# Attention blocks transposed three steps behind their scores instead of two, over four score buffers, with the low part of the transposed output subtracted one step later

## What is computed

```
o_i = softmax(scores of pattern i) @ v         for (window, dilation) in ((128,1), (512,4), (2048,16))
o   = sum_i softmax_i(lse_i) * o_i             weights s_i / sum_j s_j, s_i the softmax denominators
mix = concatenate([attn, silu(layernorm(dwconv31(a * sigmoid(g))))])
x   = x + mix @ w_out
```

## Time and profile before

| | |
|---|---|
| median of 3 runs | 2429.41 us |
| the profiled execution's own time | 2427.01 us |
| its span in the trace | 2425.2 us |
| TensorE (PE) busy | 2377.7 us, 98% |
| VectorE (DVE) busy | 1547.7 us, 64% |
| ScalarE (ACT) busy | 790.5 us, 33% |
| attention stage, from the first score to the last read of a transposed output | 251.4 to 395.4 us in the first layer, 1455.8 to about 1599.5 us in the second |

### The profile page before, as it was taken

The page is one execution under the profiler, slowest core; times in us unless marked ns, Lnnn a source line. Parts: engine busy times, 40 slices in busy tenths (PEclk is TensorE's granted clock), DMA queues, the critical chain, the costliest instruction groups (busy, mean ns, idle before and its releaser), DMA issues.

```text
span 2425.2 us, 30715 instructions
## 1 busy us (share of the span) xinstructions
PE 2377.7 (98%) x11672; PEld 1945.6 (80%) x11672; DVE 1547.7 (64%) x1659; ACT 790.5 (33%) x1050; POOL 157.0 (6%) x57
## 2 busy tenths in 40 slices
PE   7999999999999999999999998999999999999999
PEld 6888777888888888888778887778888888888887
DVE  5999774665555555555749997756555555555555
ACT  4322674432222222222332227754322222222221
POOL 0122001100000000000102120011000000000000
PEclk9999999999999999999999999999999999999999
DMA  4323531121111111111112244301211111111111
GB/s 159 88 79 114 144 81 36 44 61 52 35 52 52 52 43 52 43 52 43 43 35 79 79 139 114 79 18 53 61 53 44 48 39 52 52 51 44 46 49 70
DMA packets 46676, 153.44 MB, mean 63 GB/s; under 512 B 7424, under 2 KB 10112, under 8 KB 46592
## 3 DMA queue, kind: packets, MB, share of 16 engines
q1 hardware_dynamic: 45728, 149.93, 21.3%
q10 hardware_dynamic: 864, 2.36, 0.2%
HBM read 131.02 MB, written 21.23 MB: 63 GB/s over the span
## 4 chain that ended last, share of the span: by engine, by line
PE 88%; issue 5%; DVE 3%; ACT 2%; POOLq 0%; DMA 0%; DVEq 0%; POOL 0%; SPq 0%; ACTq 0%
PE mm L484 60%; PE aux L484 20%; PE aux L642 3%; PE aux L623 2%; PE mm L596 2%; PE aux L511 1%; DVE y L1191 1%; ACT sc L926 1%; ACT pT_large L940 0%; PE aux L520 0%; DMA x<-xT 0%; POOLq L1499 0%; DVE x_lo L1117 0%; PE aux L577 0%; DVE w_lo L1105 0%
## 5 line engine op out<-in xcount | busy, mean ns | idle before, releaser
L484 PE MATMUL mm<-x_hi,w_hi 128*128 128x512 f32 x1952 | 609.4, 393 | 17.5 <-DVE x_lo L1117 11.5
L484 PE MATMUL mm<-x_hi,w_lo 128*128 128x512 f32 x1952 | 604.5, 391 | 0.0
L484 PE MATMUL mm<-x_lo,w_hi 128*128 128x512 f32 x1952 | 604.1, 391 | 0.0
L484 PEld LDWEIGHTS mm<-x_hi,w_hi 128*128 128x128 f32 x1952 | 363.9, 188 | 97.0 <-issue 12.4
L484 PEld LDWEIGHTS mm<-x_lo,w_hi 128*128 128x128 f32 x1952 | 366.9, 188 | 79.6
L484 PEld LDWEIGHTS mm<-x_hi,w_lo 128*128 128x128 f32 x1952 | 366.7, 188 | 79.0
L793 ACT ACTIVATE w_hi<-w_raw 128x1024 fp32r<-128x1024 f32 x154 | 161.9, 1058 | 659.1 <-PE mm L484 461.2
L1111 DVE TENSOR_TENSOR x<-x,aux 128x1024 f32<-128x1024 f32 x176 | 214.8, 1221 | 121.2 <-PE aux L484 111.6
L1105 DVE TENSOR_TENSOR w_lo<-w_raw,w_hi 128x1024 fp32r<-128x1024 f32 x154 | 196.6, 1282 | 54.0 <-ACT w_hi L793 50.0
L1123 DVE TENSOR_TENSOR uv<-mm,rinv 128x1024 f32<-128x1024 f32 x44 | 53.9, 1225 | 220.3 <-PE mm L484 220.1
L1191 DVE SCALAR_TENSOR_TENSOR y<-u_all,cpar,y 128x512 f32<-128x512 f32 x248 | 186.6, 765 | 0.1
(11 more groups left out here) (190 smaller groups left out, 2938.9 us busy)
## 6 DMA issues: line engine op xcount, KB each, us to landing
w_raw<-weights SPq DMA_DIRECT2D x188, 512.0 KB, 3.6
qk_scratch<-m SPq DMA_DIRECT2D x64, 128.0 KB, 2.1
qk_scratch<-o SPq DMA_DIRECT2D x64, 128.0 KB, 2.1
x_hi<-qk_scratch SPq DMA_DIRECT2D x32, 256.0 KB, 6.4
q_first<-qk_scratch SPq DMA_DIRECT2D x8, 512.0 KB, 4.6
k_hh_first<-qk_scratch SPq DMA_DIRECT2D x16, 256.0 KB, 6.0
k_ll_first<-qk_scratch SPq DMA_DIRECT2D x16, 256.0 KB, 6.5
x_hi<-qk_scratch SPq DMA_DIRECT2D x8, 512.0 KB, 4.8
```

What stands on the lines that cost most here:

```text
L484: last = pe.matmul(acc[:, cols], a, b[:, cols], start=start and n == 0, stop=stop and n == 2)
```

## The change

Everything that follows the exponential moves one step later against the scores: transposes of step n - 3 run in step n, the attends at r6, r0, r2, r4, the h fill and `read_out` at r7, `move_out` at r4, the o fills at r1 and r3. The stage has 76 steps instead of 75. The order of the fills, and with it the bank of each, stays. `add_mask(n)` writes `sc[n % 4]` and waits for the transposes of step n - 4. The four buffers have the widths of the widest step that uses them (3, 7, 4 and 8 blocks, 22 in all; before, three of 8). On VectorE alone the subtraction into `x_lo` is done one step later still, after the next step's `add_mask` and tap.

```diff
-O_AT = 24
-H_AT = 14
+O_AT = 25
+H_AT = 15
-ATTENDS = ((5, 0, 2), (7, 3, 3), (9, 1, 6), (11, 2, 7))
-LAST_STEP = STEPS + 11
+ATTENDS = ((6, 0, 2), (8, 3, 3), (10, 1, 6), (12, 2, 7))
+LAST_STEP = STEPS + 12
...
-        if 2 <= n < STEPS + 2:
-            qb = BLOCKS[(n - 2) % TB]
+        if 3 <= n < STEPS + 3:
+            qb = BLOCKS[(n - 3) % TB]
             for a in range(0, qb + 1, 4):
-                fills.append((n, "p", n - 2, a, min(a + 4, qb + 1)))
+                fills.append((n, "p", n - 3, a, min(a + 4, qb + 1)))
...
-        sc = [sb(f"sc{i}", [P, SEQ], to=attn) for i in (2, 0, 1)]
+        widest = [(max(BLOCKS[i], BLOCKS[i + 4]) + 1) * P for i in range(4)]
+        sc = [sb(f"sc{i}", [P, widest[i]], to=attn) for i in (3, 0, 1, 2)]
         sc = sc[1:] + sc[:1]
...
-                        blocks = [sc[which % 3][:, kb * P:(kb + 1) * P] for kb in range(a, z)]
+                        blocks = [sc[which % 4][:, kb * P:(kb + 1) * P] for kb in range(a, z)]
...
-                    if n == STEPS + 4:
+                    if n == STEPS + 5:
...
-                    if n == STEPS + 7:
+                    if n == STEPS + 8:
...
-                    if n >= 11 and (n - 11) % TB == 0 and n < STEPS + 11:
-                        move_out((n - 11) // TB)
+                    if n >= 12 and (n - 12) % TB == 0 and n < STEPS + 12:
+                        move_out((n - 12) // TB)
...
-                    if n >= 3:
-
-                        dve.wait_ge(pt_full, at(l, PT, LAST_FILL[n - 3] + 1))
+                    if n >= 4:
+
+                        dve.wait_ge(pt_full, at(l, PT, LAST_FILL[n - 4] + 1))
...
-                for n in range(LAST_STEP):
+                for n in range(LAST_STEP + 1):
...
                     for f in range(PT):
-                        if FILLS[f][0] == n:
+                        if FILLS[f][0] == n - 1:
                             read_turn(f)
```

More of the change, by code:

```diff
@@ L920, in exps @@
                     h, qb = n // TB, BLOCKS[n % TB]
-                    s = sc[n % 3][:, 0:(qb + 1) * P]
+                    s = sc[n % 4][:, 0:(qb + 1) * P]
                     act.wait_ge(mm_read, at(l, MM, M_SCORE + n + 3))
@@ L1313, in add_mask @@
                     dve.wait_ge(mm_full, at(l, MM, M_SCORE + n + 1))
-                    if n == 2:
+                    if n == 3:
                         dve.wait_ge(qk_stored, at(l, QK_STORES, QK_STORES + 16))
-                    if n >= 3:
-                        dve.wait_ge(pt_full, at(l, PT, LAST_FILL[n - 3] + 1))
+                    if n >= 4:
+                        dve.wait_ge(pt_full, at(l, PT, LAST_FILL[n - 4] + 1))
                     plain(dve)
-                    dve.tensor_tensor_reduce(sc[n % 3][:, 0:keys], mm[n % 2][:, 0:keys],
+                    dve.tensor_tensor_reduce(sc[n % 4][:, 0:keys], mm[n % 2][:, 0:keys],
                                              logcount[:, SEQ - keys:SEQ], -SCALE, 3e38, ALU.add, ALU.min,
```

## The result

The changed kernel took 2407.41 us (median of 4 runs, 2406.41 to 2409.03) against 2429.1 for the kernel before: 21.7 us less, ratio 0.9914 (95% interval 0.9902 to 0.9927). Forecast were 2412.3 and a range of 2406 to 2421.5. The executions of the kernel before fall into two groups, 2426.6 to 2427.6 and 2428.5 to 2430.5 us, and three of the four behind 2429.1 are of the upper one, so the 20.2 us between the two profiled executions is the safer figure.

What follows compares the result with a forecast made beforehand. TensorE was taken as the bound (88% of the span), so only its waits could be won: 8.2 us per layer in the stretches, plus 0.75 tail, less 0.4 start, 17.1 in both, giving 2412.3 us, range 2406 to 2421.5.

Steps and rivals of the forecast that it cites:

- The waits for exponentials, 1.06 per head: TensorE's waits of 0.32 and 0.74 us at the transposes in each head vanish; head falls from 15.79 to 14.73.
- The 0.07 at k0: Wait of TensorE at k0 for ScalarE's copy of the r2 transposes, 0.07 us per head, bounds 0 and 0.5.
- both paths: From the last issue of scores at r3 to k0: ScalarE's path 5.46 us, TensorE's own 5.45, called level.
- o heads 15.7: Heads with two o fills take 15.7 us instead of 17.47, bounds 15.6 and 16.6.
- Head 3 17.6 with one transpose waiting 1.9: Subtraction queues behind a tap stretched to 2.75 us, so TensorE waits 1.9; head 3 takes 17.6 instead of 18.72.
- The GpSimd sum in head 1, 0.4 lost: Stretched tap of r6 delays the mask of r7 and read_out: 0.4 us lost once per layer, bounds 0 to 1.0.
- Start, 0.4 lost: k1 of head 0 stands behind the first scores of head 1: 0.4 us lost per layer, bounds 0 to 1.
- Tail, 0.75 gained: The 1.31 us wait for the last exponential goes, transposes queue 0.56 for ScalarE's copies: 0.75 gained, bounds 0 to 1.31.
- The sum: Seven stretches fall from 116.8 to 108.6 us; with tail and start, 8.55 gained per layer, 17.1 in both.
- B: Rival: ScalarE's copy before k0 sets every head, 0.5 us in 16 heads, 8 us less gain, 2420.3; chance 0.17.
- C: Rival: lead does not grow, exponential waits return as waits of scores; 2.8 us gained, 2426.6; chance 0.12.
- D: Rival: turn bank held too long by the late subtraction, TensorE waits at transposes; 23.8 us, 2436.1; chance 0.06.

Runs made afterwards that it cites:

- e7: Changed kernel with one more ScalarE copy of 128x512 per head, just ahead of move_out, into a tile nothing reads: 2411.8 us, ratio 0.9934 to before.
- e4: Changed kernel with the three GpSimd sums all waiting for the last tap of the last tile: 2402.8 us, ratio 0.9898 to before.
- e6: Changed kernel with the subtraction two steps after its o fill instead of one: 2443.6 us, ratio 1.0062 to before.
- e1: Changed kernel with the subtraction back in the step of its o fill, lag of three and four buffers kept: 2412.4 us, ratio 0.9936 to before.
- e2: Kernel before with only the subtraction one step later, lag of two and three buffers kept: 2423.1 us, ratio 0.9981 to before.
- e3: Changed kernel with the three full-width score buffers of before, the mask waiting for transposes of step n - 3: 2422.4 us, ratio 0.9977 to before.

## Why the prediction was right, point by point

- *The waits for exponentials, 1.06 per head.* Right: a plain head was to be 14.73 plus 0.07 and is 14.69 to 14.72. The 0.07 at k0 was not there; e7 shows that there is less than 0.1 to spare. From the last issue of `scores` at r3 (271.74) to k0 (277.04) it is 5.30, where both paths had been summed to 5.45 and 5.46: over-estimated by 0.15, and level as forecast.
- *o heads 15.7.* Measured 15.75 in head 5 of the first layer and 15.99 in the second, against 17.47 before. The 15.51 of head 7 is partly luck of the cut: 0.24 of it is the scores of a next head, which the sum did not take out.
- *Head 3 17.6 with one transpose waiting 1.9.* 17.56, and 1.77 for that transpose, where 1.9 was forecast; e4 shows the stretched tap as the cause.
- *The GpSimd sum in head 1, 0.4 lost.* Mis-sized: 0.10 (14.82 to 14.72 in e4), though the tap was stretched to 2.49.
- *Start, 0.4 lost.* Wrong in sign, and so was the sign to look for, a first k1 some 0.4 later: from the first score to the first k1 it took 13.36 and takes 13.24. The scores ahead of k1 do cost 0.4 (264.43 to 264.84), but the forecast left out that an exponential is waited for here too. TensorE's waits there were 1.37 for a mask and 1.06 for an exponential, and are 1.47, 0.28 and 0.41, all for masks: 0.3 less. The other 0.3 that it takes to come out ahead was not traced.
- *Tail, 0.75 gained.* Mis-sized: from the last k1 to the first matmul after the subtraction 13.83 became 12.67, 1.16 gained. From the start of the last fifteen transposes to the attend behind them it was 3.30 (383.50 to 386.80, with the wait of 1.31) and is 2.15 (374.51 to 376.66), which is the whole of it. Weight loads wait 0.38 for ScalarE's copy there; the forecast had 0.56. What is left of the miss is that a wait shown as 1.31 costs about 1.5 from start to start.
- *The sum.* It was 8.55 per layer and came out at 9.07 for the stretches (116.84 to 107.77), 0.12 at the start and 1.16 in the tail, 10.35; in the second layer 8.84, 0.11 and 1.17, 10.12. That is 20.5 us where 17.1 were forecast. The miss is the last three terms (0.3 + 0.5 + 0.4 per layer) and, in the first layer, 0.35 in the plain heads and 0.14 in the o heads, all to the same side. The median missed by more, 4.9 us: on the scale of the profiled execution it was 3.1 (2409.9 against 2406.8), and the 2.4 added from there to the median was 0.6 this time.
- *Rivals.* B needed 0.5 per head at k0 and found none, but e7 shows how near it was. C is out: scores in plain heads wait for no mask. (Its price had a slip: 7 of 8.55 lost leaves 1.55 per layer, 3.1 us and 2426.3, not 2.8 and 2426.6; no chance hangs on it.) D is out for this change, and e6 shows that it is real one step further: slower than the kernel before.

- *The parts.* I summed lag and postponement as if the one's worth did not hang on the other. For the sum it made no difference, since both were in my list; e1 and e2 show that in the o heads 5 and 7 either alone brings little.

Head 5 of the second layer took 15.99, where the first layer's took 15.75. There the transposes of r2 also waited for the bank: the scores ahead of them start at 1531.09 and the transposes at 1532.12, 1.03 apart, where head 1 has 0.78. The forecast had that bank free 0.1 before it is asked for. The delay comes from further ahead: in the second layer the mask of r3 starts 1.64 after its scores begin (1526.65 to 1528.29) and in the first 1.41 (332.95 to 334.36), and exponential, copy and subtraction behind it are late by as much. VectorE was idle before that mask in both; why it starts later in one layer stays open.

## What to carry to other kernels

When TensorE waits in the middle of a software pipeline, first list what each step holds (score buffer, PSUM bank, a place in an engine's list), since a resource given back later may cost nothing up to a point and then more than its own wait: here the subtraction one step late cost next to nothing except in head 3, two steps late 36 us. A deeper lag may want a further buffer, the more so where something else on the same engine is postponed; here three buffers instead of four cost 4 us alone and 15 with it. And once the slack is used, look again at contention that was covered before: moving three GpSimd sums was worth 2.5 us ahead of the change and 3.8 after it.

## What the hardware showed that was not expected

TensorE's clock fell after some waits of about 2 to 3 us. In head 3 of e6, after 2.91 us of waiting, the granted clock was 0.68 of full speed in the next 1.7 us and 0.54 in the 2.5 behind (near the lower of its levels, 1.2 and 2.4 GHz), and the k3 attend took 1.1 us longer. After 1.77 us in the changed kernel it stayed at 1.00, in both layers. Between them it went either way. In e3 the same transpose waited 2.16 in both layers. In the first, k3 took 1.53 and the head 19.59; in the second, 2.41 and 21.18. The second layer, timeline of PE and then the clock:

```profile
1505.19 0.33 PE L624 MATMUL aux<-ident,sc 128*128 128x128 f32 x1 [2.16 <-DVEq L1334]
...
1507.06 2.41 PE L643 MATMUL aux<-pT_large,sb_ 128*64 128x128 f32 x22
```
```profile
1502.00:1504.00 2.00, 1.03 (x4) 0.51 (x4) 2.00 (x1) 1.73 (x5) 1.94 (x1) 1.00 0.02 4
1504.00:1510.00 6.00, 4.81 (x34) 3.99 (x35) 2.32 (x4) 2.49 (x5) 0.00 (x0) 0.72 0.00 0
```

From that transpose to the seven transposes behind k3 it is 2.63 in the first layer and 4.21 in the second, so the fall cost 1.6 us beyond the wait (21.18 less 19.59), which no list of durations at full clock contains. In e6 the same distance is 4.21, 3.92, 4.21, 3.97, 4.21 and 3.92 in its six heads with o fills, after waits of 2.15 to 2.91: the clock fell in each, and cost 8.7 us in all. It fell once more after a second wait of 2.42 (head 5, first layer: 0.50 from 349.7 to 351.5, another 1.8 us with what was left of the first fall), while after the five other second waits, of 2.42 and 1.76, the clock was 1.00. So the clock is more than the whole of the 7 us lost beyond the 29 expected, and the waits themselves came out about 3 us below the estimate. What decides between the two outcomes at equal waits no run here shows.
